# Preparing the first queries, keys, zero rows and constants of attention inside the projection stage

## What is computed

```
proj = h @ w_in                      # fq, fk, fv, f_logit, dq, dk, dv
# forgetting attention, 8 heads of 64
s = q @ k.T * 64**-0.5 + c[q] - c[k];  s = where(mask, s, -inf);  o = softmax(s) @ v
# differential attention, 4 heads of 2 x 64, values of 128
s_n = q_n @ k_n.T * 64**-0.5 - slope * (qpos - kpos)          # n = 0, 1
lam = exp(sum(lq1 * lk1)) - exp(sum(lq2 * lk2)) + lam_init
o = rmsnorm((softmax(s_0) - lam * softmax(s_1)) @ v, g_sub) * (1 - lam_init)
```

## Time and profile before

| | us |
|---|---|
| median of three executions | 3114.57 (3112.12 to 3116.22) |
| the profiled execution, its own time | 3114.19 |
| its span, first to last instruction | 3112.0 |
| TensorE busy | 2928.1 (94%) |
| VectorE busy | 1678.8 (54%) |
| ScalarE busy | 1024.7 (33%) |
| POOL busy | 1001.7 (32%) |
| mean granted clock of TensorE | 0.979 |

### The profile page before, as it was taken

The page is one execution under the profiler, slowest core; times in us unless marked ns, Lnnn a source line. Parts: engine busy times, 40 slices in busy tenths (PEclk is TensorE's granted clock), DMA queues, the critical chain, the costliest instruction groups (busy, mean ns, idle before and its releaser), DMA issues. The chain is left out here.

```text
span 3112.0 us, 39322 instructions
## 1 busy us (share of the span) xinstructions
PE 2928.1 (94%) x14082; PEld 2411.7 (77%) x14082; DVE 1678.8 (54%) x2507; ACT 1024.7 (33%) x1974; POOL 1001.7 (32%) x734
## 2 busy tenths in 40 slices
PE   7999999698998999987997999999999999999996
PEld 5888888577877877776886788888887788888885
DVE  5211111289899898896553544444447544444446
ACT  4121111287786786874222111111111111111111
POOL 4220020147457475572113212122225222212124
PEclk9999999899999999998998999999999999999998
DMA  5343342634433344213752110111126101111112
GB/s 170 126 145 102 113 137 95 147 86 102 117 87 95 81 114 104 60 49 132 207 157 75 55 54 30 50 54 54 54 76 210 66 27 54 54 54 36 45 69 93
DMA packets 205240, 282.78 MB, mean 91 GB/s; under 512 B 12032, under 2 KB 135168, under 8 KB 205120
## 3 DMA queue, kind: packets, MB, share of 16 engines
q1 hardware_dynamic: 150256, 213.06, 23.7%
q10 hardware_dynamic: 54096, 67.38, 6.1%
q0 software_dynamic: 768, 0.79, 0.1%
HBM read 196.38 MB, written 84.80 MB: 90 GB/s over the span
## 5 line engine op out<-in xcount | busy, mean ns | idle before, releaser
L1883 DVE TENSOR_TENSOR ml_y<-ml_y,ml_ps_y 128x512 f32<-128x512 f32 x512 | 351.7, 687 | 232.8 <-PE ml_ps_y L1943 228.0
L1939 PE MATMUL ml_ps_y<-ml_dn_hi,ml_u_hi 128*128 128x512 f32 x1024 | 403.4, 394 | 13.3 <-DVE ml_y L1883 13.3
L1918 PE MATMUL ml_ps_u<-h_rows_hi,ml_up_hi 128*128 128x512 f32 x1024 | 400.2, 391 | 14.3 <-POOL ml_up_lo L1736 14.3
L1941 PE MATMUL ml_ps_y<-ml_dn_lo,ml_u_hi 128*128 128x512 f32 x1024 | 400.0, 391 | 0.0
L1943 PE MATMUL ml_ps_y<-ml_dn_hi,ml_u_lo 128*128 128x512 f32 x1024 | 399.9, 390 | 0.0
L1921 PE MATMUL ml_ps_u<-h_rows_hi,ml_up_lo 128*128 128x512 f32 x1024 | 399.8, 390 | 0.0
L1920 PE MATMUL ml_ps_u<-h_rows_lo,ml_up_hi 128*128 128x512 f32 x1024 | 399.7, 390 | 0.0
L1163 DVE TENSOR_REDUCE at_nmax<-at_ps_s 128x1 f32<-128x1024 f32 (+7 forms) x384 | 347.3, 907 | 47.2 <-PE at_ps_s L1268 42.8
L1859 DVE TENSOR_TENSOR ml_relu<-ml_relu 128x512 f32<-128x512 f32 x128 | 94.5, 738 | 498.8 <-ACT ml_relu L1822 498.8
L1736 POOL TENSOR_TENSOR ml_up_lo<-ml_up_raw,ml_up_hi 128x1024 fp32r<-128x1024 f32 x64 | 166.3, 2617 | 507.3 <-ACT ml_up_hi L1802 507.3
L1743 POOL TENSOR_TENSOR ml_dn_lo<-ml_dn_raw,ml_dn_hi 128x1024 fp32r<-128x1024 f32 x64 | 153.1, 2413 | 535.4 <-ACT ml_dn_hi L1812 535.4
(11 more groups left out here) (211 smaller groups left out, 5704.5 us busy)
## 6 DMA issues: line engine op xcount, KB each, us to landing
qk<-pj_out_sb ACTq DMA_DIRECT2D x64, 512.0 KB, 2.8
ml_up_raw<-in_w_up_dram SPq DMA_DIRECT2D x32, 1024.0 KB, 5.6
ml_dn_raw<-in_w_down_dram SPq DMA_DIRECT2D x32, 1024.0 KB, 7.6
at_q<-qk SPq DMA_DIRECT2D x96, 256.0 KB
at_k<-qk SPq DMA_DIRECT2D x96, 256.0 KB
vals<-pj_out_sb ACTq DMA_DIRECT2D x32, 512.0 KB, 3.0
at_v_sb<-vals SPq DMA_DIRECT2D x32, 512.0 KB, 3.9
pj_raw<-in_w_in_dram SPq DMA_DIRECT2D x24, 512.0 KB, 3.9
```

Source lines behind the costliest of these rows:

```text
L1883: dve.tensor_tensor(y[:, t, cols], y[:, t, cols], ps_y[:, b % 4, :], ALU.add)\
L1918: pe.matmul(ps_u[:, b % 4, :], up_hi[:, k, cols], h_hi[:, k, rows], start=(k == 0), stop=False)
L1939: pe.matmul(ps_y[:, b % 4, :], u_hi[:, s, f, rows], dn_hi[:, f, cols], start=(f == 0), stop=False)
L1941: pe.matmul(ps_y[:, b % 4, :], u_hi[:, s, f, rows], dn_lo[:, f, cols], start=False, stop=False)
```

## The change

A new class `Lasting` holds what lives through both stages. `out_sb` and the first half of the transposed input, `h_early` (high and low part of positions 0 to 1023), take the same SBUF as attention's `p_hi`, `p_lo`, `q1`, `q2`, `k1` and `k2`; the other half is `h_late`. In the projection `held` picks the half. Once the eighth of the last 16 values jobs is multiplied (`early_done`), nothing reads `h_early` any more: POOL clears the rows of `q2` and `k2`, and SyncE loads the queries of the first two query groups and the first two key pieces, while the last eight jobs run. The identity, the mask and the small constants are made by POOL in the projection behind the last `scale_row`, directly in their final form; SyncE issues the five small loads behind the gate logits' loads; VectorE and ScalarE work out lambda and the gain at jobs `carry_job` + 2, + 4 and + 6. SyncE's waits for all stores leave the end of the projection and go, as `wait_projected`, ahead of its first load for a group of heads after the first, and ahead of ScalarE's first write to `p_hi`. In `attend` the preparation and TensorE's wait for it go away, and so does the second load of ScalarE's table.

```diff
+class Lasting:
...
+    def __init__(self, nc, ctx):
+        with ExitStack() as first:
+            r = Room(nc, first, "pj")
+            self.out_sb = r.sb("out_sb", [P, 4, 1024], F32R)
+            self.h_early = r.sb("h_early", [P, 2, KT, S // 2], F32R)
+        r = Room(nc, ctx, "at")
+        self.p_hi = r.sb("p_hi", [P, 4, 512], F32R)
+        self.p_lo = r.sb("p_lo", [P, 4, 512], F32R)
+        self.q1 = r.sb("q1", [P, 2, 2, 512], F32R)
+        self.q2 = r.sb("q2", [P, 2, 2, 512], F32R)
+        self.k1 = r.sb("k1", [P, 6, 2, 512], F32R)
+        self.k2 = r.sb("k2", [P, 6, 2, 512], F32R)
...
+        self.stored = [r.sem(f"stored{s}") for s in range(4)]
+        self.rows_stored = r.sem("rows_stored")
+        self.q_loaded = [r.sem(f"q_loaded{n}") for n in range(2)]
+        self.k_loaded = [r.sem(f"k_loaded{n}") for n in range(6)]
+
+
+def load_query(sp, b, keep, qk, q_rows):
+
+    n, cols = b.qb % 2, slice(512 * b.J, 512 * b.J + 512)
+    src = qk[(0 if b.kind == FOX else 8) + b.i, :, :, cols].rearrange("z (s r) n -> z r s n", s=2)
+    sp.dma_start(f32(keep.q1[0:64, n]), src[0]).then_inc(keep.q_loaded[n], 16)
+    sp.dma_start(f32(keep.q1[64:P, n]), src[1]).then_inc(keep.q_loaded[n], 16)
+    sp.dma_start(f32(keep.q2[64:P, n]), src[0]).then_inc(keep.q_loaded[n], 16)
+    if b.kind == FOX:
+        sp.dma_start(f32(keep.q2[0:4, n]), q_rows[:, 2 * b.i:2 * b.i + 2, cols]).then_inc(keep.q_loaded[n], 16)
+    else:
+        for s in range(2):
+            sp.dma_start(f32(keep.q2[0:4, n, s]), q_rows[:, FOX_HEADS + b.i, cols]).then_inc(keep.q_loaded[n], 16)
+
+
+def load_keys(sp, u, p, n, keep, qk, k_rows):
+
+    kind, i, cols = u % 2, u // 2, slice(512 * p, 512 * p + 512)
+    src = qk[(4 if kind == FOX else 12) + i, :, :, cols].rearrange("z (s r) n -> z r s n", s=2)
+    sp.dma_start(f32(keep.k1[0:64, n]), src[0]).then_inc(keep.k_loaded[n], 16)
+    sp.dma_start(f32(keep.k1[64:P, n]), src[0]).then_inc(keep.k_loaded[n], 16)
+    sp.dma_start(f32(keep.k2[64:P, n]), src[1]).then_inc(keep.k_loaded[n], 16)
+    if kind == FOX:
+        sp.dma_start(f32(keep.k2[0:4, n]), k_rows[:, 2 * i:2 * i + 2, cols]).then_inc(keep.k_loaded[n], 16)
+    else:
+        for s in range(2):
+            sp.dma_start(f32(keep.k2[0:4, n, s]), k_rows[:, FOX_HEADS + i, cols]).then_inc(keep.k_loaded[n], 16)
+
+
+def project(nc, keep, x, g_pre_mix, w_in, b_forget, lams, g_subln, qk, vals, q_rows, k_rows):
...
+    early_done = next(m for m, job in enumerate(jobs) if job.what == "val" and job.n == DIFF and job.rb == RT // 2 - 1)
+    blocks = attention_blocks()
+    early_queries = [next(b for b in blocks if b.qb == q) for q in range(2)]
+    out_sb, stored, rows_stored = keep.out_sb, keep.stored, keep.rows_stored
...
         eps = r.sb("eps", [P, 1])
-        h_hi = r.sb("h_hi", [P, KT, S], F32R)
-        h_lo = r.sb("h_lo", [P, KT, S], F32R)
+        h_late = r.sb("h_late", [P, 2, KT, S // 2], F32R)
         raw = r.sb("raw", [P, 2, KT, P])
         w_hi = r.sb("w_hi", [P, 2, KT, P], F32R)
         w_lo = r.sb("w_lo", [P, 2, KT, P], F32R)
-        out_sb = r.sb("out_sb", [P, OR, 1024], F32R)
+        lam_in = r.sb("lam_in", [P, 4, HD])
...
+        def held(z, row, rows):
+
+            half = keep.h_early if row < S // 2 else h_late
+            at = row % (S // 2)
+            return half[:, z, :, at:at + rows]
...
+            for n, v in enumerate(lams):
+                sp.dma_start(lam_in[:, n, :], v[0:1, :].to_broadcast([P, HD])).then_inc(const_loaded, 16)
+            sp.dma_start(keep.gsub[:, :], g_subln.rearrange("o d -> d o")).then_inc(const_loaded, 16)
             for piece in range(4, len(pieces)):
                 load_piece(piece)
-            for s in range(OR):
-                sp.wait_ge(stored[s], 16 * sum(1 for job in jobs if job.out is not None and job.out % OR == s))
+            for job in jobs:
+                if job.what == "qk" and job.n in (0, 4):
+                    sp.wait_ge(stored[job.out % OR], 16 * (job.out // OR + 1))
             sp.wait_ge(rows_stored, ROWS)
+            sp.wait_ge(multiplied, early_done + 1)
+            sp.wait_ge(cleared, 1)
+            load_query(sp, early_queries[0], keep, qk, q_rows)
+            sp.wait_ge(cleared, 2)
+            load_keys(sp, 0, 0, 0, keep, qk, k_rows)
+            load_query(sp, early_queries[1], keep, qk, q_rows)
+            load_keys(sp, 0, 1, 1, keep, qk, k_rows)
...
+            for t in (keep.ident_r, keep.mask_q):
+                pool.memset(f32(t[:, :]), 0.0).then_inc(const_pool, 1)
+            pool.memset(keep.mean[:, :], 1.0 / P).then_inc(const_pool, 1)
+            pool.memset(keep.half_power[:, :], -0.5).then_inc(const_pool, 1)
+            pool.memset(keep.inverse[:, :], -1.0).then_inc(const_pool, 1)
+            pool.wait_ge(const_pool, 2)
+            for t, op, fill in ((keep.ident_r, ALU.not_equal, 1.0), (keep.mask_q, ALU.is_ge, MASKED)):
+                pool.affine_select(out=t[:, :], in_=f32(t[:, :]), compare_op=op, fill=fill,
+                                   base=0, pattern=[[-1, P]], channel_multiplier=1).then_inc(const_pool, 1)
...
+            pool.wait_ge(multiplied, early_done + 1)
+            pool.memset(f32(keep.q2[0:64, :, :, :]), 0.0).then_inc(cleared, 1)
+            pool.memset(f32(keep.k2[0:64, :, :, :]), 0.0).then_inc(cleared, 1)
...
+                if m == carry_job + 4:
+                    act.wait_ge(const_dve, 2)
+                    act.activation(keep.lam_s[:, 2:4], keep.lam_s[:, 0:2], ACT.Exp).then_inc(const_act, 1)
...
+                if m == carry_job + 2:
+                    dve.wait_ge(const_pool, 7)
+                    dve.wait_ge(const_loaded, 80)
+                    lam_v = lam_in[:, :, :].rearrange("p (a b) d -> p a b d", b=2)
+                    dve.tensor_tensor(lam_v[:, :, 0, :], lam_v[:, :, 0, :], lam_v[:, :, 1, :], ALU.mult)\
+                       .then_inc(const_dve, 1)
+                    dve.wait_ge(const_dve, 1)
+                    dve.tensor_reduce(keep.lam_s[:, 0:2], lam_v[:, :, 0, :], AX.X, ALU.add).then_inc(const_dve, 1)
+                if m == carry_job + 6:
+                    dve.wait_ge(const_act, 1)
+                    dve.tensor_tensor(keep.nlam[:, :], keep.lam_s[:, 3:4], keep.lam_s[:, 2:3], ALU.subtract)\
+                       .then_inc(const_dve, 1)
+                    dve.wait_ge(const_dve, 3)
+                    dve.tensor_scalar(keep.nlam[:, :], keep.nlam[:, :], LAM_INIT, None, ALU.subtract)\
+                       .then_inc(const_dve, 1)
+                    dve.tensor_scalar(keep.gsub[:, :], keep.gsub[:, :], 1.0 - LAM_INIT, None, ALU.mult)\
+                       .then_inc(const_dve, 1)
...
                 elif job.what == "qk":
-                    rows = slice(job.rb * 512, (job.rb + 1) * 512)
+                    h_hi, h_lo = (held(z, job.rb * 512, 512) for z in range(2))
                     s = job.n % 2
                     pe.wait_ge(w_ready, piece_at["qk", job.n] + 1)
                     for k in range(lo, hi):
-                        pe.matmul(acc[:, job.bank, :], w_hi[:, s, k], h_hi[:, k, rows], start=(k == 0), stop=False)
-                        pe.matmul(acc[:, job.bank, :], w_hi[:, s, k], h_lo[:, k, rows], start=False, stop=False)
-                        last = pe.matmul(acc[:, job.bank, :], w_lo[:, s, k], h_hi[:, k, rows],
+                        pe.matmul(acc[:, job.bank, :], w_hi[:, s, k], h_hi[:, k], start=(k == 0), stop=False)
+                        pe.matmul(acc[:, job.bank, :], w_hi[:, s, k], h_lo[:, k], start=False, stop=False)
+                        last = pe.matmul(acc[:, job.bank, :], w_lo[:, s, k], h_hi[:, k],
                                          start=False, stop=(k == KT - 1))
...
-def attend(nc, qk, vals, q_rows, k_rows, lams, g_subln, mixT):
+def attend(nc, keep, qk, vals, q_rows, k_rows, mixT):
...
+        outs = sum(1 for job in projection_jobs() if job.out is not None)
+
+        def wait_projected(eng):
+
+            for s in range(4):
+                eng.wait_ge(keep.stored[s], 16 * ((outs + 3 - s) // 4))
+
         @block.sync
         def _(sp):
+            differential = False
             for what, arg in steps:
...
+            differential = False
             for what, arg in steps:
+                if not differential and what in ("load_k", "load_v", "load_q"):
+                    differential = (arg.u if what == "load_q" else arg[0]) > 0
+                    if differential:
+                        wait_projected(sp)
                 if what == "load_k":
                     u, p = arg
-                    kind, i, n = u % 2, u // 2, k_slot(u, p)
                     held = u - (2 if p < 2 else 1)
                     if held >= 0:
                         sp.wait_ge(scored, max(sc.g for sc in scores if blocks[sc.b].u == held
                                                and sc.lo < 512 * (p + 1) and sc.lo + sc.width > 512 * p) + 1)
-                    else:
```

(70 more changed lines are left out.)

82 lines of the change are left out of this document (22 added, 60 removed).

## The result

The changed kernel takes **3093.67 us** in the median of four executions (3092.24 to 3096.10), against 3113.48 for the kernel before: a ratio of 0.994, 95% interval 0.9927 to 0.9952, so 15 to 23 us less. The forecast was 3091.0, range 3087.5 to 3096.0, faster with a chance of 0.96. A second series gave 3093.70 against 3112.97 (0.9939). The profiled execution took 3092.24, its span 3090.2.

What follows compares the result with a forecast made beforehand. TensorE, busy 94% of the span, was taken as the bound, so only its gaps could give time. Handoff 17.4 + constants 3.8 + clock 1.2 + queue 1.0 = 23.4 us, giving 3091 us on the median, range 3087.5 to 3096.

Steps and rivals of the forecast that it cites:

- The handoff: Projection's end to attention's first score: first score at 580.3 instead of 597.71, saving 17.4 us (ends 17.7 and 14.5).
- Rival 3: At the block's end, a new wait for stores or something hidden keeps 583.2: 3091 + 2.9; chance 0.12.
- The constants: Start of attention: first maximum follows its score by 0.75 instead of 4.57 us, saving 3.8 (lower end 3.1).
- The clock and the queue: Attention's opening: TensorE's clock perhaps holding, 1.2 us (nothing to 3.5); third query group no longer late, 1.0 (0 to 1.6).
- rival 2: Attention's opening: clock falls in or before first scores, stays low about 10 us; 21.5 us saved, 3093.1; chance 0.2.
- My argument from the shorter gap: Before the first score: the gap shrinks from 19.6 to 2.2 us, less than the 3 us after which the clock fell.
- The bound of 3.5 us: Attention's opening: a clock that holds at full speed is worth from nothing to 3.5 us.
- The halved layout of the transposed input, same matmuls: 0: Projection: splitting the transposed input into halves leaves the matmuls the same and costs 0 us.
- Rival 6: Projection: the halves' stride and other addresses slow its matmuls; at 25 ns each, 3126; chance 0.02.
- The bounds of my terms: Whole kernel: the terms' bounds put the time 17.6 to 26.6 us less than 3114.6.

Runs made afterwards that it cites:

- the second execution: The changed kernel run again, unaltered, against the kernel before: 3093.70 us, ratio 0.9939.
- the aligned kernel: The changed kernel with 64 bytes of padding behind the lasting constants: 3089.05 us, ratio 0.9923 to the kernel before; again 3087.86 us, 0.9920.

## Why the prediction was right, and where it was not

**The handoff: right.** 17.24 us measured by the gap of 19.64 against 2.40, 17.4 forecast. Given back alone, the wait for the stores costs 3.2 and clearing and loads 15.0, together 1.0 more than both at once; I did not settle why. Rival 3, a wait at the block's end that the trace of before hides, did not occur.

**The constants: right, at the lower end.** 4.57 - 1.44 = 3.13 us, the value given for the lower clock; in the second execution, with the clock still up, 4.57 - 0.84 = 3.73. As a price alone the term misleads: put back alone they cost 13.7, taken out together with the wait for the stores, but with clearing and loads left where they were, they are worth next to nothing. Handoff and constants were two series side by side; each covers the other. The sum was right only because the change takes out both.

**The clock and the queue: 1.6 for 2.2.** From the first maximum to the first scaled output 28.93 became 27.34. The wait of 1.63 on the third queries is gone, which would leave the clock term nearly nothing in this execution: rival 2, the cold opening, came true in its mechanism. The Trainium skill (TensorE: Matmul & The Clock Gate, Part 1) has the throttled clock as the default that activity releases; the trace agrees, with 0.50 over 10 us of an opening in which TensorE was busy 3.80 of 5.00 us at first and then 5.01 of 5.20, before the clock came back, and 1.00 when matmuls were added. My argument from the shorter gap did not hold: the clock fell 2.3 us behind the last projection matmul's end here, 4.7 behind it in the second execution, 3.0 and 3.9 in the aligned ones, against 3.0 in the kernel before. Whether the gap or the thin scores behind it bring the fall isn't shown, since the added matmuls filled both. The bound of 3.5 us held: the runs show 0.4 to 2.4.

**The step that failed: "The halved layout of the transposed input, same matmuls: 0".** It measured +5.9 and +5.2 us (583.58 and 582.87 against 577.68), 5.3 by the job times, and the padding alone took it away. Rival 6 had the mechanism, slower matmuls by "other addresses", at 25 ns each; it was up to 7 ns on part of them. (Its count of 1386 leaves out the 768 matmuls of the value jobs, which the projection also runs behind 90 us.) What I held against it, that `h_hi` and `h_lo` at different addresses run alike, was no evidence: those two are 65536 bytes apart, and equal modulo 512 with each other and with the weights. That the time still fell into the range is in part luck. The opening gave 22.0 of 23.4, but the room up to 3096 had been given for a cold clock and a wait at the block's end, not for this; and the kernel before came out at 3113.48 in the comparison, 1.1 below the 3114.57 I had started from. (The bounds of my terms, 17.6 to 26.6 less than 3114.6, give 3088.0 to 3097.0, so the range of 3087.5 to 3096 didn't quite hold them.) Without this step the time would be 3089, where the aligned kernel is: 23.9 and 23.5 us below the kernel before on the same chips.

## What to carry to other kernels

When tensors are laid out anew, compare the start addresses of a matmul's two operands modulo 512 before and after, and look at the beat of an unchanged loop in the trace: 7 ns a matmul is hard to see in one row and comes to 5 to 13 us in this stage. A series that ends "just behind" another is not priced by the distance between them; given back each alone, the two cost 13.7 and 22.3 us here, together far more than the whole (23.9). And ask behind each removed wait which queue sets the next one.

## What the runs showed that I had not expected

- 64 unused bytes cost 12.7 us in the kernel before: most jobs of 24 matmuls of 512 columns took 5.60 us (233 ns each) in place of 5.44 (227 ns). So it was, within 0.03 us, with stationary and moving operand 32 or 128 bytes apart modulo 512. In both profiled executions of the changed kernel the job times agree to 0.01 us.
- A block's end with nothing outstanding leaves TensorE without work for 2.37 to 2.40 us, of which copy, subtraction and store issue of the last job take 1.8 (the matmul ends at 583.58 + 0.39 = 583.97, the issues at 584.02 + 1.71 = 585.73). That leaves 0.4 to SyncE's next issue at 586.15 and 0.6 to the first score.
- Behind a load of 0.5 KB, issued beside values and keys on another queue, VectorE waited until 9.8 us after the issue (586.27 to 596.10).
